# Norm by token after the product: the first layer's inputs reach the multiplier without their square roots

## The chip, the cores and the metric

The kernel runs on one core of one Trainium2 chip. The metric is the device time of one execution in microseconds, the median of several runs. The core's engines work side by side, each in the order of its own program, and meet at semaphores: TensorE (PE in the rows) multiplies, VectorE (DVE), ScalarE (ACT) and GpSimd (POOL) do elementwise work, SyncE (SP) issues most of the DMA transfers.

## What is computed

Two transformer blocks over 256 tokens of 1024 channels. Only the start of the first matters here:

```
def rms_norm(x, g):
    y = xf * lax.rsqrt(jnp.mean(xf * xf, axis=-1, keepdims=True) + EPS)
    return (y * g)
u = rms_norm(h, norm_mix[i])
m = rms_norm(mem, norm_mem[i])
mk, mv = jnp.split(m @ w_mem_kv[i], 2, axis=-1)
q, k, v, f_logit, mq = jnp.split(u @ fox_w_in[j], ...)
q = rms_norm(q.reshape(B, S, FOX_HEADS, HEAD_DIM), fox_g_q[j])
k = rms_norm(k.reshape(B, S, FOX_HEADS, HEAD_DIM), fox_g_k[j])
log_f = jax.nn.log_sigmoid((f_logit + fox_b_f[j]).astype(jnp.float32))
mix = forget_attention(q, k, v, log_f)
mem_out = memory_attention(mq, mk, mv, g_mq[i], g_mk[i])
```

Behind it come the output product, a SwiGLU, a second layer (convolution, memory attention, eight experts of which each token takes two) and the second block. Every `rms_norm` divides a token by the root of its mean square plus EPS = 1e-6. A token's divisor is the same for all its channels.

## The kernel before

**Weights in units.** All dense weights are cut into units of 128 x 2048 fp32 (1 MB) that stream through a ring of six buffers, `raw`. A unit is split into a rounded part `wh` (ScalarE, `split_hi`, line 837) and the rest `wl` (VectorE, `split_lo`, line 2074), in three buffers, and the tokens likewise into `xh` and `xl`. A product is three matmuls a step (lines 1371 to 1373, `exact`): 48 matmuls of 256 columns for one of these first units. SP loads unit n as soon as unit n - 6 is split on VectorE. `split_after(name)` stands in the programs of ScalarE and VectorE and splits the unit three places behind `name`; ScalarE's part of it waits until the product `name` is done, since it takes its buffer.

**The order of the first layer.** The units are mk0 and mv0 (keys and values of the memory), mq0 (queries to the memory), then fq0, fk0, fv0, fq1 and so on, so unit 7 is fk1. PE's program before them: 20 filler matmuls on zeros (`idle_start`, line 1513), the sum of the squares of the memory with a matrix of ones (`norm_sum(0)`, line 1394), 16 more fillers (line 1508), mk0, the sum of the squares of x (`norm_sum(1)`), a two-column product for lambda, mv0, the head sums of mk0 (`head_sum(0)`, line 1431), the gate product (`by_heads`, line 1483) with its transpose by token (line 1531), mq0, and the spread of mk0's head roots over channels (`head_spread(0)`, line 1442). mk0 and mq0 take their tokens tile by tile as they arrive (`ready=arriving(...)`), with k as the outer loop over the eight tiles of 128 channels.

**The norms.** ScalarE squares the tokens (line 854), PE sums them, ScalarE takes the root over all 128 x 256 places (`norm_sd`, line 859), VectorE the reciprocal (line 2100) and then the product token x weight x reciprocal, tile by tile (`norm_raw`, line 2067); ScalarE rounds each tile (`norm_hi`, line 880) and VectorE subtracts. `qk_square`, `head_sum`, `qk_sd` (line 902), a reciprocal with a copy (lines 2150 and 2151) and `head_spread` do the same by head behind each of the eight products of queries and keys; `values_out` (line 913) takes a value product out of PSUM. ScalarE's `slot(h)` puts these steps beside the attention, two slots to a unit.

**Side work.** `rn_mem`, the memory's reciprocals, is used once more far behind, for the second layer's memory. The gates go ScalarE, VectorE, ScalarE, then as negated sums to DRAM and back to all partitions on GpSimd's own queue (lines 711 and 700), where GpSimd adds masks (line 707). Ahead of unit 7, SP also writes zeros over `x_rows` and `y_rows` in DRAM (`zero_rows`, lines 637 and 639, 6 MB and 2.5 MB).

## Time and profile before

| what | value |
|---|---|
| median of three runs | 1816.58 us (1816.5 to 1817.22) |
| the profiled execution | 1819.06 us |
| its span, first to last instruction | 1817.2 us |
| mean granted TensorE clock | 0.989 of full |
| busy: PE, VectorE, ScalarE, GpSimd | 98%, 78%, 64%, 13% |

The profile is one execution. It has a page with busy times and groups of instructions, and a trace that can be asked for a timeline, for stretches and for single lines. PE records each fp32 matmul twice, so its counts are double. In a timeline neighbours of the same kind are merged, and the time in brackets is the idle time ahead. An engine's wait counts only where PE, in the end, waits for it.

### The profile page before, as it was taken

What the parts mean: (1) busy time and instruction counts of PE and PEld (TensorE: products, weight loads), DVE (VectorE), ACT (ScalarE), POOL (GpSimd) and SP (SyncE); (2) the same over time, 40 slices, a digit from 0 to 9 for tenths busy, and PEclk for the clock granted to TensorE, in tenths of its full rate; (3) what the DMA queues carried; (4) which work ended last, traced back from release to release, by engine and by line L of the source; (5) the groups of instructions that cost most, each with busy time, mean ns of one, the idle gap of its engine ahead of it and who ended that gap; (6) DMA issues with size and microseconds to landing.
All of it is one profiled execution on the core that took longest, in us unless ns stands there. A gap on an engine that the chain in (4) does not pass through costs nothing.

```text
span 1817.2 us, 28018 instructions
## 1 busy us (share of the span) xinstructions
PE 1788.5 (98%) x10770; PEld 1589.9 (87%) x10770; DVE 1412.7 (78%) x1342; ACT 1164.4 (64%) x1148; POOL 232.5 (13%) x194
## 2 busy tenths in 40 slices
PE   9999999999999999999999999999999999899998
PEld 8988999998988888888888888888887899799998
DVE  6665977689778888888888889888889867665554
ACT  6775434457677777777777777777777767543332
POOL 0452111302030000000000000000007002302221
PEclk9999999999999999999999999999999999999999
DMA  9734888841379999999999999999999953235540
GB/s 392 274 121 139 323 337 324 319 147 35 128 280 383 368 387 376 368 396 373 386 390 365 389 382 367 388 372 396 375 363 422 381 186 139 87 119 179 180 158 24
DMA packets 75695, 523.27 MB, mean 288 GB/s; under 512 B 8328, under 2 KB 8480, under 8 KB 15072
## 3 DMA queue, kind: packets, MB, share of 16 engines
q1 hardware_dynamic: 73344, 514.02, 74.1%
q0 software_dynamic: 2272, 8.15, 1.2%
q8 instruction: 56, 0.92, 0.2%
q14 instruction: 23, 0.19, 0.0%
HBM read 506.38 MB, written 15.75 MB: 287 GB/s over the span
## 4 chain that ended last, share of the span: by engine, by line
PE 92%; DVE 4%; ACT 2%; issue 1%; DMA 0%; POOL 0%; DVEq 0%; SPq 0%; ACTq 0%
PE ps L1371 27%; PE ps L1373 27%; PE ps L1372 27%; PE ps L1704 2%; DVE wl L2074 2%; PE ps L1863 1%; PE ps L1385 1%; PE ps L1552 1%; DVE sqz L2067 1%; ACT wh L837 1%; PE ps L1569 1%; PE ps L1401 0%; PE ps L1394 0%; DMA big<-in_mem 0%; PE ps L1871 0%
## 5 line engine op out<-in xcount | busy, mean ns | idle before, releaser
L2074 DVE TENSOR_TENSOR wl<-raw,wh 128x2048 fp32r<-128x2048 f32 x446 | 1026.6, 2304 | 251.5 <-ACT wh L837 138.8
L1189 ACT ACTIVATE wh<-raw 128x2048 fp32r<-128x2048 f32 x335 | 642.8, 1919 | 179.3 <-PE ps L1373 179.3
L1371 PE MATMUL ps<-wh,xh 128*128 128x512 f32 (+1 forms) x1040 | 396.5, 381 | 2.4 <-DVE wl L2074 2.4
L1373 PE MATMUL ps<-wh,xl 128*128 128x512 f32 (+1 forms) x1040 | 390.1, 375 | 0.0
L1372 PE MATMUL ps<-wl,xh 128*128 128x512 f32 (+1 forms) x1040 | 389.6, 375 | 0.0
L1371 PE MATMUL ps<-xh,wh 128*128 128x256 f32 x1120 | 323.1, 288 | 5.5 <-DVE xl L2074 3.7
L1372 PE MATMUL ps<-xl,wh 128*128 128x256 f32 x1120 | 318.5, 284 | 0.0
L1373 PE MATMUL ps<-xh,wl 128*128 128x256 f32 x1120 | 318.5, 284 | 0.0
L837 ACT ACTIVATE wh<-raw 128x2048 fp32r<-128x2048 f32 x108 | 206.3, 1911 | 174.4 <-PE ps L1373 170.6
L1371 PEld LDWEIGHTS ps<-wh,xh 128*128 128x128 f32 x1040 | 195.8, 188 | 38.8 <-DVE wl L2074 4.0
L1373 PEld LDWEIGHTS ps<-wh,xl 128*128 128x128 f32 x1040 | 195.7, 188 | 35.7
L1372 PEld LDWEIGHTS ps<-wl,xh 128*128 128x128 f32 x1040 | 196.0, 188 | 34.0 <-issue 0.5
L1371 PEld LDWEIGHTS ps<-xh,wh 128*128 128x128 f32 x1120 | 216.7, 193 | 9.4 <-issue 6.8
L1372 PEld LDWEIGHTS ps<-xl,wh 128*128 128x128 f32 x1120 | 216.5, 193 | 0.5 <-issue 0.5
L1373 PEld LDWEIGHTS ps<-xh,wl 128*128 128x128 f32 x1120 | 216.4, 193 | 0.0
L1371 PE MATMUL ps<-wh,ah 128*128 128x512 f32 x448 | 175.8, 392 | 0.0
L1373 PE MATMUL ps<-wh,al 128*128 128x512 f32 x448 | 174.6, 390 | 0.0
L1372 PE MATMUL ps<-wl,ah 128*128 128x512 f32 x448 | 174.5, 389 | 0.0
L1371 PE MATMUL ps<-ah,wh 128*128 128x256 f32 x496 | 142.4, 287 | 1.0 <-POOL al L747 0.9
L1372 PE MATMUL ps<-al,wh 128*128 128x256 f32 x496 | 140.8, 284 | 0.0
L1373 PE MATMUL ps<-ah,wl 128*128 128x256 f32 x496 | 140.8, 284 | 0.0
L747 POOL TENSOR_TENSOR al<-att_p,ah 128x512 fp32r<-128x512 f32 x27 | 74.6, 2762 | 333.9 <-ACT ah L1051 333.9
(327 smaller groups left out, 1960.8 us busy)
## 6 DMA issues: line engine op xcount, KB each, us to landing
raw<-in_experts SPq DMA_DIRECT2D x336, 1024.0 KB, 6.8
raw<-in_units SPq DMA_DIRECT2D x134, 1024.0 KB, 5.3
x_rows<-big SPq DMA_DIRECT2D x1, 6144.0 KB, 35.6
big<-x_rows SPq DMA_DIRECT2D x8, 512.0 KB, 7.8
y_rows<-big SPq DMA_DIRECT2D x7, 512.0 KB, 8.2
y_rows<-big SPq DMA_DIRECT2D x1, 2560.0 KB, 41.3
sqz<-gate_rows POOLq DMA_DIRECT2D x12, 192.0 KB, 4.4
big<-in_mem SPq DMA_DIRECT2D x1, 1024.0 KB, 7.1
```

What stands on the lines that cost most here:

```text
L747: pool.tensor_tensor(al[:, c % 2, :], sg[:, c % 2, :], ah[:, c % 2, :].bitcast(F32), ALU.subtract).then_inc(sem("hid_lo"), 1)
L837: act.activation(wh[:, p % SPL, :], raw[:, n % RAW, :], ACT.Copy).then_inc(sem("hi_ready"), 1)
L1189: act.activation(wh[:, p % SPL, :], raw[:, n % RAW, :], ACT.Copy).then_inc(sem("hi_ready"), 1)
L1371: mm(out_, lh, rh, start=start, stop=False, **kw)
L1372: mm(out_, lh, rl, start=False, stop=False, **kw)
L1373: return mm(out_, ll, rh, start=False, stop=stop, **kw)
L1385: ins = pe.transpose(bank(name)[:, at:at + P], src, ident)
L1552: ins = mm(s[:, at:at + nk], m["q"][:, P * t:P * t + P], m["k"][:, 0:nk], start=True, stop=True)
L1569: mm(o, m["v"][0], pT[:, 0:T], start=True, stop=False, skip_group_check=True)
L1704: mm(bank(f"conv{c}")[:, 0:T], diag[:, n % DIAG_RING, :], upad[:, c, tap:tap + T], start=(tap == 0), stop=(n + 1 == taps_through(PE_CONV, ...
L1863: ins = pe.transpose(psum[:, P * f:P * f + P], sg[:, c % 2, P * f:P * f + P], ident)
L2074: return V.tensor_tensor(out_, whole, leading.bitcast(F32), ALU.subtract)
```

## The change

The first layer no longer divides tokens before the products. `xh` and `xl` are made from token x norm weight alone: ScalarE's `weighted_hi` rounds that product, VectorE's `weighted_lo` subtracts. What was left out is a factor by token, and it is put back where a token's row is small:

- queries and keys are normed by head anyway, so there the factor cancels except in EPS; `qk_sd` now adds EPS x (mean square + EPS) by token (`tok_eps`) and takes two instructions, one for each half of the tokens;
- values (`values_scaled_out`, two instructions for one) and gate logits (VectorE, two for one) are multiplied by the token's reciprocal `tok_r`;
- the sums of squares come by token (four matmuls of one column each for x and the memory) behind mv0, of squares that VectorE has added up first; the squares of the memory are GpSimd's, which did nothing there before, those of x ScalarE's;
- the gate product takes x itself against weights times norm weights (`gate_w`), by token at once: 16 matmuls of 12 columns in place of 8 of 256 and a transpose;
- `rn_mem`, needed later, comes from two more transposes on PE and a copy on ScalarE.

mk0's and mv0's units and the memory are loaded, split and multiplied in halves, the load order is new (`cols` early, the constants late), the second filler is gone and the first has 18 matmuls.

```diff
-            load(0)
-            sp.dma_start(flat(mem0), mem_dram).then_inc(sem("ld_mem"), 16)
+            first = main_dram[0:1, :, :].rearrange("a p f -> p (a f)")
+            sp.dma_start(raw[:, 0, 0:HALF], first[:, 0:HALF]).then_inc(sem("first_half_loaded"), 16)
+            sp.dma_start(cols[:, :], cols_dram).then_inc(sem("ld_cols"), 16)
+            sp.dma_start(flat(mem0)[:, 0:HALF], mem_dram[:, 0:HALF]).then_inc(sem("ld_mem"), 16)
+            sp.dma_start(raw[:, 0, HALF:UW], first[:, HALF:UW]).then_inc(sem("ring_loaded0"), 16)
+            sp.dma_start(flat(mem0)[:, HALF:UW], mem_dram[:, HALF:UW]).then_inc(sem("ld_mem_rest"), 16)
+            load(1)
+            sp.dma_start(flat(hT), x_dram).then_inc(sem("ld_x"), 16)
             sp.dma_start(cst[:, 0:C_ROT], cst_dram[:, 0:C_ROT]).then_inc(sem("ld_cst"), 16)
-            sp.dma_start(cols[:, :], cols_dram).then_inc(sem("ld_cols"), 16)
-            sp.dma_start(flat(hT), x_dram).then_inc(sem("ld_x"), 16)
...
+            for j in range(4):
+                pool.wait_ge(sem("ld_mem" if j < 2 else "ld_mem_rest"), 16)
+                pool.tensor_tensor(sqz[:, 512 * j:512 * j + 512], pair_of(mem0, j), pair_of(mem0, j),
+                                   ALU.mult).then_inc(sem("mem_sq"), 1)
...
+            def split_hi_half(p, half):
+
+                if (p, half) == (0, 0):
+                    act.wait_ge(sem("first_half_loaded"), 16)
+                else:
+                    wait_loaded(act, p)
+                at = slice(HALF * half, HALF * half + HALF)
+                act.activation(wh[:, p, at], raw[:, p, at], ACT.Copy).then_inc(
+                    sem("hi_ready" if half else "hi_half_ready"), 1)
...
+            def weighted_hi(src, at, k):
+
+                act.activation(xh[:, k, :], src[:, k, :], ACT.Copy,
+                               scale=cols[:, at + k:at + k + 1]).then_inc(sem("norm_hi"), 1)
...
+                    act.activation(rq[:, k % 2, :], bank(f"qsum{k}")[:, 0:8], ACT.Sqrt, scale=1.0 / HD,
+                                   bias=eps).then_inc(drained(f"qsum{k}"), 1)
+                    return
+                of = int(k > 0)
+                act.wait_ge(sem("tok_eps_ready"), of + 1)
+                roots, sums = (v.rearrange("p (a t n) -> p a t n", a=2, t=TT)
+                               for v in (rq[:, k % 2, :], bank(f"qsum{k}")[:, 0:8]))
+                for t in range(TT):
+                    ins = act.activation(roots[:, :, t, :], sums[:, :, t, :], ACT.Sqrt, scale=1.0 / HD,
+                                         bias=tok_eps[:, of, t:t + 1])
+                ins.then_inc(drained(f"qsum{k}"), 1)
...
+            def values_scaled_out(name, dst, of):
+
+                wait_done(act, name)
+                act.wait_ge(sem("tok_r_ready"), 1)
+                for t in range(TT):
+                    ins = act.activation(dst[:, t, :], bank(name)[:, T * t:T * t + T], ACT.Copy,
+                                         scale=tok_r[:, of, t:t + 1])
+                ins.then_inc(drained(name), 1)
...
+            split_hi_half(0, 0)
+            act.wait_ge(sem("ld_cols"), 16)
             act.wait_ge(sem("ld_mem"), 16)
+            for k in range(2):
+                weighted_hi(mem0, V_MEM, k)
+            split_hi_half(0, 1)
+            for k in range(2, KT):
+                if k == 4:
+                    act.wait_ge(sem("ld_mem_rest"), 16)
+                weighted_hi(mem0, V_MEM, k)
+            split_hi_half(1, 0)
+            split_hi_half(1, 1)
+            act.wait_ge(sem("ld_x"), 16)
             for j in range(4):
-                square(mem0, sqz, j)
+                act.activation(x_sq[:, 512 * j:512 * j + 512], pair_of(hT, j), ACT.Square).then_inc(sem("norm_sq"), 2)
+            split_hi(2)
             act.wait_ge(sem("ld_cst"), 16)
             warm(ACT.Sqrt)
-            norm_sd(0, rn_mem)
-            norm_hi("mem0", mem0)
-            act.wait_ge(sem("ld_x"), 16)
-            for j in range(4):
-                square(hT, x_sq, j)
-            split_hi(1)
-            norm_sd(1, rn)
-            split_hi(2)
             qk_square(0)
             split_after("mk0")
             wait_done(act, "mv0")
-            norm_hi("x")
-            wait_filled(act, "foxf")
-            act.activation(forget, bank("foxf")[0:FOX_HEADS, 0:T], ACT.Copy).then_inc(drained("foxf"), 1)
+            for k in range(KT):
+                weighted_hi(hT, V_MIX, k)
+            qk_sd(0)
+            act.wait_ge(sem("tok_eps_ready"), 2)
+            act.activation(flat(tok_r), flat(tok_ms), ACT.Sqrt).then_inc(sem("tok_sd"), 1)
             split_after("mv0")
             wait_filled(act, "nsum1")
-            values_out("mv0", vv[:, :, FOX:D])
-            qk_sd(0)
+            values_scaled_out("mv0", vv[:, :, FOX:D], 0)
...
+                        values_scaled_out(name, vv[:, :, at:at + T], 1)
                     if h == 5:
                         qk_spread(0)
+                        wait_filled(act, "memr")
+                        act.activation(rn_mem[:, :], bank("memr")[:, 0:T], ACT.Copy).then_inc(drained("memr"), 1)
                     elif FOX_UNITS[u - 1] in QK_UNITS:
                         qk_spread(QK_UNITS.index(FOX_UNITS[u - 1]))
                     split_after(name)
                 if h == 7:
...
                 claim(pe, name)
                 steps = [(t, k) for k in range(KT) for t in range(2)] if ready else [(t, k) for t in range(2) for k in range(KT)]
                 for t, k in steps:
+                    if halves and (t, k) == (0, KT // 2):
+                        pe.wait_ge(sem("lo_ready"), POS[name] + 1)
...
-            for _ in range(20):
+            for _ in range(18):
                 mm(bank("idle_start")[:, 0:P], idle_tile, idle_tile, start=True, stop=True)
+            by_channels("mk0", ready=arriving("mem0"), halves=True)
+            by_tokens("mv0", halves=True)
+
             pe.wait_ge(sem("ld_cst"), 16)
-            norm_sum(0)
-            keep_running("idle_mem0", 16)
-            by_channels("mk0", ready=arriving("mem0"))
-            norm_sum(1, x_sq)
-
+            claim(pe, "nsum1")
+            pe.wait_ge(sem("x_sq_added"), 3)
+            for c in range(2):
+                ins = add_by_token(1, c, x_sq, 0, 1)
+            ins.then_inc(filled("nsum1"), 1)
+            claim(pe, "nsum0")
+            pe.wait_ge(sem("mem_sq_added"), 3)
+            for c in range(2):
+                ins = add_by_token(0, c, sqz, 0, 1)
+            ins.then_inc(filled("nsum0"), 1)
+            claim(pe, "flT")
+            pe.wait_ge(sem("gate_w_ready"), 1)
+            pe.wait_ge(sem("ld_x"), 16)
+            for k in range(KT):
+                for t in range(TT):
+                    at = FOX_HEADS * t
+                    ins = mm(bank("flT")[:, at:at + FOX_HEADS], hT[:, k, P * t:P * t + P], gate_w[:, k, :],
+                             start=(k == 0 and t == 0), stop=(k == KT - 1), skip_group_check=True)
+            ins.then_inc(filled("flT"), 1)
+            head_sum(0)
             pe.wait_ge(sem("lam_prod"), 2)
             claim(pe, "lam")
             mm(bank("lam")[:, 0:2], ones, lam[:, 0:2], start=True, stop=True).then_inc(filled("lam"), 1)
-            by_tokens("mv0")
-            head_sum(0)
-
-
-            pe.wait_ge(sem("ld_cols"), 16)
-            by_heads("foxf", cols[:, V_WF:V_RT].rearrange("p (k n) -> p k n", k=KT), FOX_HEADS, "x")
-            claim(pe, "flT")
-            for t in range(TT):
-                ins = mm(bank("flT")[:, FOX_HEADS * t:FOX_HEADS * t + FOX_HEADS], forget[:, P * t:P * t + P],
-                         ident[0:FOX_HEADS, 0:FOX_HEADS], start=True, stop=True)
-            ins.then_inc(filled("flT"), 1)
+
             by_channels("mq0", ready=arriving("x"))
             head_spread(0)
+            claim(pe, "memr")
+            pe.wait_ge(sem("tok_r_ready"), 1)
+            for t in range(TT):
+                ins = pe.transpose(bank("memr")[:, P * t:P * t + P], tok_r[:, 0, t:t + 1].broadcast_to([P, P]), ident)
+            ins.then_inc(filled("memr"), 1)
...
+                dve.wait_ge(sem("hi_ready" if half else "hi_half_ready"), p + 1)
+                at = slice(HALF * half, HALF * half + HALF)
+                rest(wl[:, p, at], raw[:, p, at], wh[:, p, at]).then_inc(
+                    sem("lo_ready" if half else "lo_half_ready"), 1)
...
+            def weighted_lo(name, src, at, k):
+
+                wait_hi(dve, name, k)
+                stt(xl[:, k, :], src[:, k, :], col(at + k), xh[:, k, :].bitcast(F32), ALU.mult,
+                    ALU.subtract).then_inc(sem("norm_lo_dve"), 1)
...
+            def token_means(k, of):
+
+                wait_filled(dve, f"nsum{k}")
+                V.tensor_scalar(tok_ms[:, of, :], bank(f"nsum{k}")[:, 0:TT], 1.0 / D, EPS, ALU.mult,
+                                ALU.add).then_inc(drained(f"nsum{k}"), 1)
+                wait_drained(dve, f"nsum{k}")
+                V.tensor_scalar(tok_eps[:, of, :], tok_ms[:, of, :], EPS, None, ALU.mult).then_inc(sem("tok_eps_ready"), 1)
...
-            split_lo(0)
+            split_lo_half(0, 0)
             dve.wait_ge(sem("ld_cols"), 16)
+            for k in range(2):
+                weighted_lo("mem0", mem0, V_MEM, k)
+            split_lo_half(0, 1)
+            for k in range(2, KT):
+                weighted_lo("mem0", mem0, V_MEM, k)
+            split_lo_half(1, 0)
+            split_lo_half(1, 1)
+            V.tensor_tensor(gate_w, cols[:, V_WF:V_RT].rearrange("p (k n) -> p k n", k=KT),
+                            cols[:, V_MIX:V_MIX + KT].unsqueeze(2).broadcast_to([P, KT, FOX_HEADS]),
+                            ALU.mult).then_inc(sem("gate_w_ready"), 1)
+            for j in (1, 2, 3):
+                dve.wait_ge(sem("norm_sq"), 2 * (j + 1))
+                if j > 1:
+                    dve.wait_ge(sem("x_sq_added"), j - 1)
+                V.tensor_tensor(x_sq[:, 0:512], x_sq[:, 0:512], x_sq[:, 512 * j:512 * j + 512],
+                                ALU.add).then_inc(sem("x_sq_added"), 1)
+            for j in (1, 2, 3):
+                dve.wait_ge(sem("mem_sq"), j + 1)
+                if j > 1:
+                    dve.wait_ge(sem("mem_sq_added"), j - 1)
+                V.tensor_tensor(sqz[:, 0:512], sqz[:, 0:512], sqz[:, 512 * j:512 * j + 512],
+                                ALU.add).then_inc(sem("mem_sq_added"), 1)
+            split_lo(2)
...
-            split_lo(1)
-            norm_rms(1, rn)
-            norm_raw(hT, gains(V_MIX), rn[:, :])
-            split_lo(2)
-            norm_lo("x")
+            for k in range(2):
+                weighted_lo("x", hT, V_MIX, k)
+            token_means(0, 0)
+            token_means(1, 1)
+            for k in range(2, KT):
+                weighted_lo("x", hT, V_MIX, k)
             split_after("mk0")
+            dve.wait_ge(sem("tok_sd"), 1)
+            V.reciprocal(flat(tok_r), flat(tok_r)).then_inc(sem("tok_r_ready"), 1)
+            head_root(0)
...
             wait_filled(dve, "flT")
-            V.tensor_tensor(lsf[:, 0, :, :], bank("flT")[:, 0:2 * FOX_HEADS].rearrange("p (a b) -> p a b", a=2),
-                            cols[:, V_BF:V_BF + FOX_HEADS].unsqueeze(1).broadcast_to([P, TT, FOX_HEADS]),
-                            ALU.add).then_inc(drained("flT"), 1)
+            dve.wait_ge(sem("tok_r_ready"), 1)
+            for t in range(TT):
+                ins = stt(lsf[:, 0, t, :], bank("flT")[:, FOX_HEADS * t:FOX_HEADS * t + FOX_HEADS], tok_r[:, 1, t:t + 1],
+                          cols[:, V_BF:V_BF + FOX_HEADS], ALU.mult, ALU.add)
+            ins.then_inc(drained("flT"), 1)
```

The first rows of PE's program. Before, `ps<-sqz,cst` is the first sum of squares and `ps<-cst` the second filler:

```order
L1513 MATMUL ps<-att_pT 128x128 x20
L1394 MATMUL ps<-sqz,cst 128x256 x8
L1508 MATMUL ps<-cst 128x128 x16
L1371 MATMUL ps<-xh,wh 128x256
L1372 MATMUL ps<-xl,wh 128x256
L1373 MATMUL ps<-xh,wl 128x256
```

The same place in the changed kernel, with the semaphores that each row waits for:

```order
L1553 MATMUL ps<-att_pT 128x128 [waits idle_tile]
L1553 MATMUL ps<-att_pT 128x128 x17
L1421 MATMUL ps<-xh,wh 128x256 [waits norm_lo_dve,lo_half_ready]
L1422 MATMUL ps<-xl,wh 128x256
L1423 MATMUL ps<-xh,wl 128x256
L1421 MATMUL ps<-xh,wh 128x256
```

The sum and the second filler went from ahead of the first product, which now waits for half a unit (`lo_half_ready`) and a tile (`norm_lo_dve`).

PE's program between mv0 and mq0. Before, `att_pT` holds the squares of mk0, `cols` the gate weights and `att_p` the gate product:

```order
L1371 MATMUL ps<-wh,xh 128x256
L1372 MATMUL ps<-wl,xh 128x256
L1373 MATMUL ps<-wh,xl 128x256
L1431 MATMUL ps<-cst,att_pT 128x2 x4
L1483 MATMUL ps<-sqz,cols 12x256 x8
L1531 MATMUL ps<-cst,att_p 128x12 x2
L1371 MATMUL ps<-xh,wh 128x256
```

The same place in the changed kernel, where `big` and `sqz` hold the added squares of x and of the memory and `plan_f` the weighted gate weights:

```order
L1422 MATMUL ps<-wl,xh 128x256
L1423 MATMUL ps<-wh,xl 128x256
L1445 MATMUL ps<-cst,big 128x1 x4
L1445 MATMUL ps<-cst,sqz 128x1 x4
L1574 MATMUL ps<-plan_f,hT 128x12 x16
L1475 MATMUL ps<-cst,att_pT 128x2 x4
L1580 MATMUL ps<-lam,cst 128x2
L1421 MATMUL ps<-xh,wh 128x256
```

The sums by token stand here now, the gate product has 16 small matmuls and no transpose, and the lambda product came down from ahead of mv0.

VectorE's program from its start. Before, `gq` and `lam` are small constants and `rn_mem` the memory's reciprocals:

```order
L2074 TENSOR_TENSOR wl<-raw,wh 128x2048
L2171 TENSOR_SCALAR gq<-cols 128x1
L2172 TENSOR_SCALAR gq<-cols 128x2
L2174 TENSOR_TENSOR lam<-cols 128x1
L2175 TENSOR_TENSOR lam<-lam,cst 128x1
L2176 TENSOR_TENSOR lam<-lam,cst 128x1
L2100 RECIPROCAL rn_mem<-rn_mem 128x256
L2067 SCALAR_TENSOR_TENSOR big<-big,cols,rn_mem 128x256 x3
L2074 TENSOR_TENSOR xl<-big,xh 128x256
L2067 SCALAR_TENSOR_TENSOR big<-big,cols,rn_mem 128x256
```

The same place in the changed kernel:

```order
L2127 TENSOR_TENSOR wl<-raw,wh 128x1024
L2120 SCALAR_TENSOR_TENSOR xl<-big,cols,xh 128x256 x2
L2127 TENSOR_TENSOR wl<-raw,wh 128x1024
L2120 SCALAR_TENSOR_TENSOR xl<-big,cols,xh 128x256 x6
L2127 TENSOR_TENSOR wl<-raw,wh 128x1024 x2
L2251 TENSOR_TENSOR plan_f<-cols 128x96
L2258 TENSOR_TENSOR big<-big 128x512 x3
L2264 TENSOR_TENSOR sqz<-sqz 128x512 x3
L2127 TENSOR_TENSOR wl<-raw,wh 128x2048
L2268 TENSOR_SCALAR gq<-cols 128x1
```

The tiles of the memory come directly behind half a unit, without a reciprocal, and six additions of squares came in ahead of the next whole unit.

## Rows read from the trace of the kernel before

**Rows 1.** the page, first part: busy us, share of the span, instructions
```profile
PE 1788.5 (98%) x10770; PEld 1589.9 (87%) x10770; DVE 1412.7 (78%) x1342; ACT 1164.4 (64%) x1148; POOL 232.5 (13%) x194
```

**Rows 2.** PE's timeline: start us, us, engine line op out<-in xcount
```profile
0.97 7.33 PE L1513 MATMUL ps<-att_pT 128*128 128x128 f32 x40 [0.97 <-POOL att_pT L693]
9.02 3.69 PE L1394 MATMUL ps<-sqz,cst 128*128 128x256 f32 x16 [0.72 <-ACT sqz L854]
16.80 0.55 PE L1371 MATMUL ps<-xh,wh 128*128 128x256 f32 x1 [2.34 <-DVE xl L2074]
...
24.07 3.62 PE L1394 MATMUL ps<-big,cst 128*128 128x256 f32 x16
...
33.51 0.95 PE L1431 MATMUL ps<-cst,att_pT 128*128 128x2 f32 x8
34.38 3.62 PE L1483 MATMUL ps<-sqz,cols 128*12 128x256 f32 x16
...
39.01 0.39 PE L1371 MATMUL ps<-xh,wh 128*128 128x256 f32 x1
...
44.87 0.60 PE L1442 MATMUL ps<-cst,rq_by_head 128*128 128x128 f32 x4
...
51.95 0.60 PE L1442 MATMUL ps<-cst,rq_by_head 128*128 128x128 f32 x4
...
69.45 0.60 PE L1442 MATMUL ps<-cst,rq_by_head 128*128 128x128 f32 x4
```

**Rows 3.** stretches: span, busy of each engine (x), PEclk, DMA share, GB/s
```profile
19.00:20.00 1.00, 1.00 (x7) 1.00 (x6) 1.00 (x4) 0.42 (x1) 0.00 (x0) 0.50 1.02 426
20.00:21.00 1.00, 1.00 (x10) 1.00 (x10) 0.98 (x3) 0.99 (x3) 0.00 (x0) 0.95 1.03 426
```

**Rows 4.** timelines of ScalarE and SP, one DMA issue (KB, us to landing)
```profile
5.75 1.91 ACT L837 ACTIVATE wh<-raw 128x2048 fp32r<-128x2048 f32 x1 [3.75 <-DMA raw<-in_units]
8.24 2.19 ACT L854 ACTIVATE sqz<-big 128x512 f32<-128x512 f32 x4 [0.59 <-DMA big<-in_mem]
...
10.86 21.50 SPq L639 DMA_DIRECT2D y_rows<-big  x1
...
raw<-in_units SPq DMA_DIRECT2D x1, 1024.0 KB, 22.2
```

**Rows 5.** GpSimd's L747 (duration min/median/max ns), then timelines of both
```profile
L747 POOL TENSOR_TENSOR al<-att_p,ah x27: 1288/2879/2889, 185.6 to 1796.9; 128x512 fp32r<-128x512 f32 x27
...
201.98 2.63 POOL L747 TENSOR_TENSOR al<-att_p,ah 128x512 fp32r<-128x512 f32 x1 [13.53 <-ACT ah L1051]
203.74 3.01 DVE L2074 TENSOR_TENSOR wl<-raw,wh 128x2048 fp32r<-128x2048 f32 x1 [0.30 <-ACT wh L837]
...
357.79 2.31 DVE L2074 TENSOR_TENSOR wl<-raw,wh 128x2048 fp32r<-128x2048 f32 x1 [3.10 <-ACT wh L837]
357.91 2.78 POOL L690 TENSOR_TENSOR xl<-sqz,xh 128x256 fp32r<-128x256 f32 x1
```

**Rows 6.** timelines of four engines, one row of DMA issues
```profile
30.02 3.26 DVE L2067 SCALAR_TENSOR_TENSOR sqz<-hT,cols,rn 128x256 f32<-128x256 f32 x8
...
33.71 2.56 ACT L880 ACTIVATE xh<-sqz 128x256 fp32r<-128x256 f32 x8 [1.41 <-PE ps L1373]
...
61.82 1.92 ACT L837 ACTIVATE wh<-raw 128x2048 fp32r<-128x2048 f32 x1
...
66.16 1.28 ACT L902 ACT_TABLE_LOAD   x1
...
sqz<-gate_rows POOLq DMA_DIRECT2D x5, 192.0 KB, 5.5
...
67.96 3.93 POOL L707 TENSOR_TENSOR sqz<-sqz,cst 128x128 f32<-128x128 f32 x10 [3.29 <-DMA sqz<-gate_rows]
...
68.45 0.57 DVE L2151 COPY rq_by_head<-rq 128x512 f32<-128x512 f32 x1
...
74.48 0.60 PE L1385 MATMUL ps<-cst,att_p 128*128 128x128 f32 x4
```

More of the change, by code:

```diff
@@ L640, in zero_rows @@
                              zeros.broadcast_to([P, MAXBLK + 2 - E, D])).then_inc(sem("rows_zeroed"), 16)
-            for n in range(1, U0):
+            for n in range(2, U0):
                 if n == NUMBER["fk1"]:
@@ L1444, in head_spread, with by_channels @@
                 ins.then_inc(filled(f"qrms{k}"), 1)
-            def by_channels(name, nb=None, ready=None, half_done=None):
-                h, l = weights(name, KT, nb)
+            def by_channels(name, nb=None, ready=None, half_done=None, halves=False):
+                h, l = weights(name, KT, nb, halves)
                 claim(pe, name)
@@ L1470, in by_tokens @@
                     for k in range(KT):
+                        if halves and (t, k) == (0, KT // 2):
+                            pe.wait_ge(sem("lo_ready"), POS[name] + 1)
                         c = slice(P * t, P * t + P)
```

51 lines of the change are left out of this document (19 added, 32 removed).

## The prediction

> **What bounds the kernel now.** I read the busy times first: PE is busy for 1788.5 of 1817.2 us [rows 1], so time can come only from PE instructions that vanish and from the 28.7 us in which PE has none. The change touches the first 75 us, so next came PE's timeline from the start. The filler of 20 small matmuls (40 records, the hardware runs each in two) ends at 8.3, the sum of the memory's squares runs from 9.02 to 12.7, a second filler to 14.5, then PE has nothing for 2.3 us, and the first product, mk0, starts only at 16.80 [rows 2]. Ahead of it lie the square root, the reciprocal and the multiplication by it. After mk0 comes the sum of the squares of x at 24.07, then mv0, the head sums at 33.51, the gate product of 3.62 us at 34.38, a wait and its transpose until 39.01, where mq0 starts; the spread behind mq0 stands at 44.87, the next two that I use at 51.95 and 69.45 [rows 2]. From 39 to 69.45 PE has no gap. The granted clock is 0.50, so 1.2 GHz, in mk0's first 3.2 us, just after the 2.3 us of nothing: still 0.50 from 19 to 20 and 0.95 from 20 to 21, with 7 matmuls in the one stretch and 10 in the other [rows 3]. So a burst after a gap has two prices.
>
> **The front of mk0.** Weights and tokens come over one DMA queue: ScalarE starts on the first MB at 5.75 and on the second at 8.24, both released by their DMA [rows 4], so 2.5 us per MB. In the new order that gives half a unit at 4.5, the columns at 5.1, half the memory at 6.4, the second halves at 7.7 and 8.9, unit 1 at 11.4, x at 13.9 and unit 2 at 16.9. The total up to unit 2 is the old one.
> ScalarE rounds 2048 columns in 1.92 and eight tiles of 256 in 2.56 [rows 6], so it has the first half at 5.5, tiles 0 and 1 by 7.1, the second half at 8.7 and tile 7 at 10.7. VectorE takes 2.3 for 2048 columns [rows 5] and 0.41 per tile (3.26 for eight [rows 6]). Alone it would have tile 0 at 7.4, tile 1 at 7.8, the second half at 10.0, tile 2 at 10.4, tile 7 at 12.5.
> It isn't alone: the four squares of the memory go to GpSimd. A 128x512 tile takes it 1.29 at least, 2.88 in the median [rows 5]. The rows show why: the tile that started at 201.98 took 2.63, and the VectorE split beside it, started at 203.74, took 3.01 in place of 2.31; the GpSimd tile at 357.91 took 2.78, until the split of 357.79 had ended [rows 5]. One waits for the other's whole instruction, and the one already waiting goes next. So I let them alternate: square 0 at 6.7 to 7.95 (behind the first weight half), tile 0 to 8.4, square 1 to 9.65, tile 1 to 10.1, square 2 to 11.35, second half to 12.5, square 3 to 13.75, tile 2 to 14.2, tile 7 at 16.2. Had GpSimd run all four first, tile 2 would stand at 14.2 too.
> The Trainium skill (SBUF — State Buffer, section "SBUF: two separate sides") says the same and goes further: GpSimd and a VectorE instruction with two SBUF inputs exclude each other for a whole instruction. The trace agrees for the splits (2.78, 3.01); by that rule the line above holds for the new tiles too, and without it tile 2 would come at 10.4.
> PE's filler of 18 ends at 7.6 (7.33 x 36/40 from 0.97 [rows 2]). Tiles 0 and 1 are short bursts at 8.4 and 10.1, then PE waits some 3.3 us for tile 2. Before, 2.3 us of nothing brought the clock down, so I take the low clock from 14.2: 15 matmuls of 0.21 in 3.2 us, as from 16.80 to 20.0 [rows 2, 3], and 21 at 0.12 (5.86 per 48, from 39.01 to 44.87 [rows 2]). **mk0 ends at 19.9**, before at 24.07. At full clock it would be 18.5, without the collisions at 14.7 to 16.3.
>
> **From mk0 to mq0.** mv0 needs unit 1 split, at 18.5, so it runs from 19.9 to 25.8. Then 8 matmuls for the two sums by token and 16 for the gates, all bound by loading 128x128 fp32 weights: 0.20 each, by the four of the head sum, which fill 33.51 to 34.38 with some overlap [rows 2]: 1.6 and 3.2. Bounds for the 16: the same as the old eight with 256 columns, 3.62, and 0.12 each, 1.9. Head sum 0.8, lambda 0.3. **mq0 starts at 31.6, before 39.01: 7.4 earlier.** Gone from PE between mk0 and mq0 are the second sum (24.07, 3.62), the gate product (3.62) and 1.0 of wait and transpose [rows 2]; the first sum and the fillers stood ahead of mk0 and are paid in its start.
> Is x ready? VectorE: unit 1 to 18.5, gate weights, six additions of 512 columns at about 0.7 (estimate from 2.3 for 2048) to 22.9, unit 2 to 25.2. ScalarE rounds x behind mv0's end, 25.8 to 28.4; VectorE's last x tile is at 31.1 at 0.41 each, behind the sums by token at 27.6. mq0 takes 0.73 per tile, so it isn't held.
>
> **What is late next.** ScalarE's queue: root for heads 31.6, unit 4 32 to 34, values 34.7 (two instructions for one, about +0.2), three table loads of 1.28 [rows 6] with the exponential and the logarithm to 39.0, squares of mq0 39.5, spread 40.0, the new copy of the memory's reciprocals 40.3, unit 5 42.2, table 43.5, root 43.9. VectorE splits unit 5 until 44.5, reciprocal and copy to 45.1. PE has mq0 to 37.5, spread 0.4, the two new transposes 0.3, fq0 and head sum to 44.7, and waits about 0.4. Its spread stands at 45.2 where it stood at 51.95 [rows 2]: **6.8 earlier**.
> The second limit is a DMA. The zeroing of y_rows blocks SP from 10.86 for 21.50 us; unit 7 is issued only then, at 32.4, and lands 22.2 later, at 54.6 [rows 4]. Nothing in the change moves these bytes: the DMA engines are full (share 1.02 [rows 3]), before and after. ScalarE starts unit 7 at 61.82 [rows 6], so it can be at most 7.2 earlier. Behind that, in order, are table loads, the root of fk0, and VectorE's copy of 0.57 at 68.45 [rows 6], which ends 0.4 ahead of PE's spread at 69.45 [rows 2]; the root is now two instructions, about +0.2. **PE can be at most about 7.4 earlier there, however fast the front is.** At 6.8 the unit is wanted at 55.0 and just doesn't wait.
> GpSimd: ten masks of gates from 67.96 take 3.93, loaded 5.5 us after issue [rows 6], and everything on that path moves with the 6.8.
> Later stages: PE waits there for its own producers, no load, so the 6.8 stays. The two-part roots and values add about 0.2 on ScalarE seven and four times; I count 0.
>
> **The sum.** The profiled execution took 1819.06 (span 1817.2), 2.5 above the median 1816.58: 1819.06 - 6.8 = 1812.3, and for the median **1809.8**.
>
> **Rivals.** (1) Forecast, 55%: 6.8, with 5.6 to 7.3 for the unknown prices (flT 1.9 to 3.6, ScalarE's added instructions): 1809.3 to 1811.0.
> (2) The collisions cost less or the clock stays up, 20%: for it, the alternation is inferred from single cases; against it, four of four squares meet busy VectorE. mq0 starts at 26.5 to 30, and unit 7 stops the gain at 7.4: 1809.2.
> (3) Neither limit holds, 6%: unit 7 lands earlier as the halves change the queue, and mq0 starts at 26.5. Gain 11 to 12: about 1805. Against it: same bytes, same queue, full at both ends.
> (4) ScalarE and VectorE queues slip more, 15%: each further us at the chain from mq0's squares to 45.1 is a us of PE, since there PE already waits. With 1.5 to 3.8 us more: gain 3.0 to 5.3, 1811.3 to 1813.6.
> (5) Slower, 4%: the gate loads. They are issued at about 55 in place of 61.9, with more ring loads open. If they queue behind these, they land as unit 7 does [rows 4], some 20 us after issue, at 75.5; masks take 3.9, and from their end at 71.9 it was 2.6 to the first transposes of probabilities at 74.48 [rows 6]. These then stand at 82, where PE wants them at 67.7: 14 us lost against 6.8 won, 1824. It decides from a landing of about 13 us on. Against it: before, while the engines were full, they landed in 5.5 [rows 6].
>
> **Chances and range.** About 0.2% (3.6 us) can be told from no change here: faster, below 1812.9, holds (1) to (3) and most of (4): 0.91; same 0.05; slower 0.04. For 8 in 10 the range takes in (1), (2) with 1.4 us for unit 7's landing, which the smaller packets may move, and most of (4), and leaves out (3) and (5): 1807.8 to 1812.6.
>
> **What would show it.** After: mk0's first matmul at 8 to 9 and tile 2's at about 14; POOL's four squares 1.3 to 2.6 each; granted clock 0.50 from about 14; mq0 at 31.6; a short wait of PE before the spread at 45; unit 7 landing at 54.6 and wanted then. A start of mq0 below 29 with the same total would prove (2); a total below 1807 would prove my unit 7 limit wrong; PE waits of over 1 us between 38 and 55 would speak for (4).

## The result and the profile after it

| | kernel before | changed kernel |
|---|---|---|
| median of 20 runs, us | 1816.59 (1813.92 to 1821.23) | 1819.16 (1816.53 to 1824.66) |
| ratio to the kernel before, 95% interval | | 1.0016 (1.0010 to 1.0023) |
| span of the profiled execution, us | 1817.2 | 1819.1 |

The forecast was 1809.8, within 1807.8 to 1812.6. The changed kernel takes 2.6 us **more**. The interval excludes a gain. The loss is small, but a second series (e12, below) gave 1.0025 (1.0014 to 1.0035).

**The front did what was forecast.** PE's timeline of the changed kernel from the start (start, us, engine, line, operation, shapes, count, in brackets the idle time before it and what ended it):

```profile
0.97 5.84 PE L1553 MATMUL ps<-att_pT 128*128 128x128 f32 x36 [0.97 <-POOL att_pT L700]
8.75 0.36 PE L1421 MATMUL ps<-xh,wh 128*128 128x256 f32 x1 [1.94 <-DVE xl L2120]
...
13.22 0.39 PE L1421 MATMUL ps<-xh,wh 128*128 128x256 f32 x1 [2.40 <-DVE xl L2120]
...
25.35 0.95 PE L1445 MATMUL ps<-cst,big 128*128 128x1 f32 x8
26.16 1.03 PE L1445 MATMUL ps<-cst,sqz 128*128 128x1 f32 x8
27.06 5.99 PE L1574 MATMUL ps<-plan_f,hT 128*128 128x12 f32 x32
32.89 1.84 PE L1475 MATMUL ps<-cst,att_pT 128*128 128x2 f32 x8
34.60 0.56 PE L1580 MATMUL ps<-lam,cst 128*128 128x2 f32 x2
42.35 0.60 PE L1486 MATMUL ps<-cst,rq_by_head 128*128 128x128 f32 x4
...
49.65 0.60 PE L1486 MATMUL ps<-cst,rq_by_head 128*128 128x128 f32 x4
...
67.16 0.60 PE L1486 MATMUL ps<-cst,rq_by_head 128*128 128x128 f32 x4
...
77.01 1.11 PE L1438 MATMUL ps<-cst,att_p 128*128 128x128 f32 x4 [4.37 <-POOL att_p L736]
```

mk0 starts at 8.75 in place of 16.80 [rows 2], memory tile 2 comes at 13.22 (forecast 14.2), mk0 ends at 19.6 (forecast 19.9), and mv0 ends at 25.35 (forecast 25.8). Then the 16 short gate matmuls (32 records) take 5.99 us, the head sum 1.84 and the lambda product 0.56, and the spread behind mq0 stands at 42.35. That is 2.5 us ahead of the 44.87 of before [rows 2], and the lead is 2.3 at the other two spreads (49.65 against 51.95, 67.16 against 69.45). Then PE stands still for 4.37 us in front of the first transposes of probabilities: they come at 77.01, before at 74.48 [rows 6].

The stretches show the clock in both places. Columns: from and to; PE, its weight loads, VectorE, ScalarE and GpSimd busy, each with its number of instructions; granted clock, DMA share, GB/s:

```profile
26.00:28.00 2.00, 2.00 (x20) 2.00 (x19) 0.95 (x3) 2.00 (x5) 0.00 (x0) 1.00 1.01 422
28.00:30.00 2.00, 2.00 (x12) 2.00 (x12) 1.96 (x8) 1.78 (x5) 0.00 (x0) 0.54 0.97 401
30.00:32.00 2.00, 2.00 (x11) 2.00 (x11) 2.00 (x4) 0.00 (x0) 0.00 (x0) 0.50 1.02 420
32.00:35.00 3.00, 3.00 (x15) 3.00 (x16) 1.01 (x1) 0.22 (x2) 0.00 (x0) 0.50 1.03 425
35.00:38.00 3.00, 3.00 (x15) 3.00 (x16) 1.58 (x4) 2.98 (x7) 0.00 (x0) 0.50 1.02 421
38.00:42.00 4.00, 4.00 (x34) 4.00 (x34) 2.06 (x5) 3.02 (x5) 0.00 (x0) 0.95 1.02 417
70.00:76.00 6.00, 2.62 (x17) 1.96 (x15) 4.44 (x6) 2.08 (x5) 4.44 (x7) 0.99 0.27 72
76.00:80.00 4.00, 2.99 (x14) 2.99 (x15) 1.51 (x4) 0.86 (x2) 2.89 (x5) 0.50 0.56 233
```

From 28 to 38 PE is counted as busy all the time, and runs at 0.50, that is 1.2 GHz. From 76 to 80, behind the wait, it is at 0.50 again.

What GpSimd does in front of those transposes, in the changed kernel's timeline of POOL:

```profile
60.17 2.75 POOL L710 DMA_DIRECT2D sqz<-gate_rows  x5 [5.57 <-DMA gate_rows<-rn]
66.64 0.78 POOL L717 TENSOR_TENSOR sqz<-sqz,cst 128x128 f32<-128x128 f32 x2 [3.71 <-DMA sqz<-gate_rows]
...
71.16 0.78 POOL L717 TENSOR_TENSOR sqz<-sqz,cst 128x128 f32<-128x128 f32 x2 [0.61 <-DMA sqz<-gate_rows]
72.89 2.25 POOL L717 TENSOR_TENSOR sqz<-sqz,cst 128x128 f32<-128x128 f32 x2 [0.95 <-DMA sqz<-gate_rows]
75.12 0.93 POOL L734 TENSOR_SCALAR att_p<-att_p,rsum 128x256 f32<-128x256 f32 x1
76.04 0.92 POOL L736 TENSOR_SCALAR att_p<-att_p,rsum 128x256 f32<-128x256 f32 x1
```

and VectorE's weight split beside the last of them:

```profile
72.23 2.27 DVE L2127 TENSOR_TENSOR wl<-raw,wh 128x2048 fp32r<-128x2048 f32 x1
```

The gate loads are issued at 60.17, 1.7 us earlier than the 61.91 of before, but land one by one, 6.3 to 10.5 us after issue (median 8.4, before 5.4 to 5.9). The last pair of masks begins at 72.89, inside VectorE's split of 72.23 to 74.50, and takes 2.25 us where the others take 0.78. The normalisation of map 0's probabilities stands behind it on GpSimd: 75.12 to 76.96. PE wanted it at 72.64. Before, the masks ran from 67.96 to 71.9 [rows 6], the normalisation until 73.70, VectorE's split began at 74.13 and PE came at 74.48: everything fitted, with 0.8 us to spare for PE and 0.4 for the split. These are the two normalisations and the split of before:

```profile
71.86 0.94 POOL L724 TENSOR_SCALAR att_p<-att_p,rsum 128x256 f32<-128x256 f32 x1
72.78 0.92 POOL L726 TENSOR_SCALAR att_p<-att_p,rsum 128x256 f32<-128x256 f32 x1
...
74.13 2.27 DVE L2074 TENSOR_TENSOR wl<-raw,wh 128x2048 fp32r<-128x2048 f32 x1
```

### The profile page after: what moved, and what is told of

Its sections match the earlier page's. It is cut to its first block, busy times and chain, and to the rows that moved or that the text cites. A ratio compares the mean times of both kernels' runs of the same rounds, so it can differ in the third digit from the quotient of the medians.

```text
span 1819.1 us, 27999 instructions
## 1 busy us (share of the span) xinstructions
PE 1784.5 (98%) x10748; PEld 1588.2 (87%) x10748; DVE 1411.5 (78%) x1339; ACT 1164.9 (64%) x1157; POOL 237.5 (13%) x198
## 4 chain that ended last, share of the span: by engine, by line
PE 90%; DVE 4%; ACT 2%; DMA 1%; issue 1%; POOL 1%; DVEq 0%; SPq 0%; ACTq 0%
PE ps L1421 27%; PE ps L1423 27%; PE ps L1422 27%; DVE wl L2127 2%; PE ps L1757 2%; PE ps L1916 1%; PE ps L1438 1%; ACT wh L847 1%; DMA sqz<-gate_rows 1%; DVE sqz L2120 1%; PE ps L1622 1%; PE ps L1605 0%; PE ps L1445 0%; DMA raw<-in_units 0%; PE ps L1924 0%
## 5 line engine op out<-in xcount | busy, mean ns | idle before, releaser
L2127 DVE TENSOR_TENSOR wl<-raw,wh 128x2048 fp32r<-128x2048 f32 (+1 forms) x448 | 1027.1, 2295 | 248.6 <-ACT wh L847 129.4
```

The lines of the kernel that those rows point to most:

```text
L2127: return V.tensor_tensor(out_, whole, leading.bitcast(F32), ALU.subtract)
```

## The experiments

One measure needs a word first. From 154 us on the kernels run the same instructions, but spells of low clock fall in other places of them in each execution, and the profiled runs drift against each other by some us until the end. Two late stretches of the kernel before, and then of the changed kernel:

```profile
1480.00:1500.00 20.00, 20.00 (x166) 19.89 (x165) 10.78 (x11) 12.26 (x14) 1.21 (x4) 1.00 0.46 159
1580.00:1600.00 20.00, 17.52 (x125) 16.57 (x124) 8.90 (x24) 8.19 (x25) 6.54 (x6) 0.91 0.16 54
```

```profile
1480.00:1500.00 20.00, 20.00 (x157) 19.89 (x157) 12.63 (x17) 11.20 (x13) 0.00 (x0) 0.94 0.36 113
1580.00:1600.00 20.00, 16.18 (x120) 14.77 (x118) 9.81 (x32) 9.32 (x29) 8.95 (x9) 1.00 0.16 54
```

The granted clock is below 1 in the second stretch of the one and in the first of the other. So the table has, beside medians and ratios, the time in the profile at which GpSimd issues the load of c_row, behind the first attention. It is a reading of one execution. The three kernels that should agree there do: before 154.42, e1 154.45, e11 154.39. Two executions of one kernel differ by more: 0.35 for the changed kernel (159.77 and 159.42), 0.81 for e4 and e8, which are the same.

| run | gate product, us | first spread | PE waits for probabilities | c_row load | median, us | ratio (95%) |
|---|---|---|---|---|---|---|
| before | 3.62 | 44.87 | 0 | 154.42 | 1816.4 to 1817.2 | 1 |
| after | 5.99 | 42.35 | 4.4 | 159.77 | 1819.16 | 1.0016 (1.0010 to 1.0023) |
| e12 after again | 6.23 | 42.09 | 4.4 | 159.42 | 1821.67 | 1.0025 (1.0014 to 1.0035) |
| e1 before, zeroing late | | 44.90 | 0 | 154.45 | 1815.66 | 0.9987 (0.9977 to 0.9998) |
| e2 after, zeroing late | 3.90 | 40.24 | 0 | 150.54 | 1814.09 | 0.9980 (0.9969 to 0.9991) |
| e3 gates by heads | 3.62 | 39.64 | 4.4 | 155.74 | 1817.96 | 1.0002 (0.9991 to 1.0012) |
| e4, e8 e2 and e3 | 3.62 | 36.67, 37.47 | 0 | 146.97, 147.78 | 1810.29, 1810.41 | 0.9958 (0.9942 to 0.9974), 0.9957 (0.9941 to 0.9974) |
| e5 wide gates | 3.79 | 38.97 | 4.4 | 155.37 | 1818.63 | 1.0000 (0.9988 to 1.0012) |
| e6 by heads, ring held | 3.62 | 37.61 | 4.4 | 155.08 | 1818.00 | 1.0002 (0.9990 to 1.0013) |
| e7 e8, squares late | 3.62 | 38.09 | 0 | 148.46 | 1811.18 | 0.9963 (0.9949 to 0.9977) |
| e9 after, probabilities first | 3.72 | 39.50 | 0 | 149.80 | 1815.44 | 0.9987 (0.9974 to 0.9999) |
| e10 e3, probabilities first | 3.62 | 38.16 | 0 | 148.46 | 1811.28 | 0.9968 (0.9959 to 0.9977) |
| e11 before, probabilities first | | 44.84 | 0 | 154.39 | 1815.62 | 0.9998 (0.9988 to 1.0008) |

(Gates "by heads" are eight matmuls of 12 stationary and 256 streamed columns, as in the kernel before, instead of 16. The changed kernel's gate product is 16 matmuls of 12 streamed columns; e2 and e9 have it unchanged, e5 streams 96. Each median is of 6 to 20 executions, each ratio is to executions of the kernel before on the same chip, and can differ by 0.001 from the quotient of the medians, as in e5.)

### First four: the queue and the clock

The profile left two theories. Q: the DMA engines are full with the zeroing of rows and the weights, so the gate loads land late however early they are asked for. C: the clock falls in the short gate matmuls. e1 and e2 move the zeroing behind later weight loads, in the kernel before and in the changed one:

```
-                if n == NUMBER["fk1"]:
+                if n == NUMBER["fo0"] + 1:
                     zero_rows()
```

> The kernel before, with the zeroing of x_rows and y_rows issued six units later (ahead of unit 13 in place of unit 7). Theory Q (queue): in the first 75 us the DMA engines are full with 8.5 MB of zeros, so whatever needs a transfer there comes at a fixed time however early it is asked for. The kernel before is late enough not to wait for any of it, so this gives the same time, within 0.1% of 1816.6. Rival P (programs): the changed kernel lost its gain on ScalarE, VectorE and GpSimd, the queue has no part; same here too. A gain of over 2 us here would be against both and would mean that the zeroing itself costs PE time.

> The changed kernel with the zeroing issued six units later. Theory Q: the five gate loads land 1.5 us apart no more but within 3 us of their issue, PE's wait of 4.4 us before the first transposes of probabilities goes, with it the low clock behind it (about 2 us), and PE keeps the lead of 2 to 2.5 us that it had at mq0: 1819.2 - 6.2 = 1813, 0.2% below the kernel before. Rival P: the gates are late from ScalarE's or VectorE's order, the wait stays, 1819.

e3 puts the gate product back into the form of before, the 12 gate columns stationary and 256 tokens streamed, with its copy and its transposes; e4 has both edits.

```
-                for t in range(TT):
-                    ins = mm(bank("flT")[:, at:at + FOX_HEADS], hT[:, k, P * t:P * t + P], gate_w[:, k, :], ...)
+                ins = mm(bank("foxf")[0:FOX_HEADS, 0:T], gate_w[:, k, :], hT[:, k, :], ...)
```

> The changed kernel, but the gate product in the old form: 8 matmuls of 256 columns with the weighted gate weights as stationary operand, a copy on ScalarE and the transpose, in place of 16 of 12 columns. Zeroing where it was. Theory C (clock): the 16 short matmuls took 5.9 us since the clock fell to 0.50 in them, and it stayed down into mq0; with 256 columns it stays at 1.00, mq0 starts at 32.5 to 33 in place of 35.0 and its spread stands at 38.8 to 39.5 in place of 42.35. With theory Q the gain is lost again at the gate loads, which land at 70 to 73 as before: total 1818 to 1820. Without Q it would be 1816. Rival to C: the short matmuls are slow by themselves (0.37 us each); then head sum and first half of mq0 are still slow here.

> Both edits: gate product by heads and zeroing late. Theories C and Q together: lead of 5.5 to 6 us at mq0's spread, no wait for gates: 1810.5 to 1811.5, near my forecast for the change. If Q is wrong: as e3.

e3 keeps the clock at 1.00 from 26 to 42, so C holds: the spread comes at 39.64 in place of 42.35. But it ends only level with the kernel before (1.0002), since the wait of 4.4 us is still there. e2 removes the wait; e4 has both gains and stands near the forecast, 6.1 us below the kernel before. But Q was too simple. In e2 the gate loads still took 8.3 us to land. What the late zeroing shortened was the two stores ahead of them (2.2 and 1.9 us to landing in place of 5.2 and 5.8), so that the loads were asked for at 54.13. And e1, in which nothing waited, shows that zeroing late is worth nothing to the chain of the kernel before (154.45).

### Next four: width, order of loads, squares

> The changed kernel, but each of the 16 gate matmuls streams 96 columns instead of 12 (the 12 gate columns eight times over, through a broadcast view; only the first copy is read). The result is the same. Theory C2 (the clock falls because only 12 columns go through behind each 128x128 weight load): with 96 columns the granted clock stays at 1.00 from 26 to 35, the 16 take 3.2 to 3.7 us in place of 5.99, the head sum 1.0 in place of 1.84, mq0 starts at about 32 in place of 35.0. The wait for the gate masks stays (theory Q): landing 8 us, PE waits 3.5 to 5; total 1816.5 to 1818.5. Rival W (what lowers the clock is any run of small matmuls with a new 128x128 stationary each, however wide): clock 0.5 from 28 to 35 again, the 16 take 5.9 or more, mq0 at 35 or later, total as the changed kernel, 1819.

```
-                             gate_w[:, k, :],
+                             gate_w[:, k, :].unsqueeze(1).broadcast_to([P, 8, FOX_HEADS]),
```

The timeline's row and the stretches of e5:

```profile
28.44 3.79 PE L1574 MATMUL ps<-plan_f,hT 128*128 128x96 f32 x32
```

```profile
28.00:30.00 2.00, 2.00 (x20) 2.00 (x20) 1.68 (x8) 2.00 (x6) 0.00 (x0) 1.00 0.97 403
30.00:32.00 2.00, 2.00 (x20) 2.00 (x20) 2.00 (x6) 0.24 (x1) 0.00 (x0) 1.00 1.02 418
32.00:35.00 3.00, 3.00 (x28) 3.00 (x27) 2.41 (x4) 1.92 (x4) 0.00 (x0) 1.00 1.03 423
```

Same weight loads, same count, eight times the columns, and the 16 take 3.79 us against 5.99. C2 holds, W falls. Width itself costs nothing here: in e9 (below) the clock stayed up until all 16 narrow ones were through, and they took 3.72:

```profile
25.92 3.72 PE L1576 MATMUL ps<-plan_f,hT 128*128 128x12 f32 x32
```

```profile
28.00:30.00 2.00, 2.00 (x19) 2.00 (x18) 1.97 (x7) 1.57 (x4) 0.00 (x0) 0.92 0.98 403
30.00:32.00 2.00, 2.00 (x10) 2.00 (x11) 2.00 (x3) 0.79 (x4) 0.00 (x0) 0.50 1.01 416
```

So something that doesn't grow with the columns sets the pace, 0.23 to 0.24 us a matmul at full clock; that it is the load of the 128x128 weights, as the forecast had it, fits but isn't shown by itself. What the width decides is the clock. All four profiles with 12 columns lose it between 27.6 and 30.0 us (changed kernel, e12, e2, e9), and none of the seven with 96 or 256 does. From the first gate matmul to the spread behind mq0 the four take 13.6 to 15.3 us, e5 10.5 and the six by heads 11.2: the low clock costs 3.0 to 4.8 us, by where it falls. Even so e5's median of 1818.63 lies just above its expected range, since its wait of 4.4 us stayed.

> The gate product by heads as in e3, and in addition SyncE issues ring unit 11 and the ones behind it only after the gates are stored, so just about when GpSimd issues its five gate loads; no bytes vanish. Theory R (the gate loads wait behind the ring loads issued ahead of them): they land 5 to 6.5 us after issue instead of 8.1, the last mask ends by 69 instead of 72.5, PE's wait for probabilities falls from 4.4 to 1 to 2.5 us, total 1814 to 1816. Rival Z (the DMA engines are behind by the zeroing and by units 7 to 10 anyway, the order of the last ones doesn't matter): landing 7.5 to 8.5, wait 3.5 to 5 us, total 1817 to 1818. Unit 11 is issued at about 60 and split behind 80, so neither expects a wait for it.

```
+                if n == 11:
+                    sp.wait_ge(sem("gate_stored"), 32)
                 load(n)
```

Landing is 8.4 us in the median, the wait 4.4, the total as in e3: by the expectation R falls. But the edit tests it only weakly. SyncE waits for the same stores as GpSimd, so unit 11 went out at 55.11, 0.3 us ahead of the first gate load, and two ring loads landed among the gate loads at 67.2 and 70.0, as in e3 (67.5 and 70.6). It doesn't exclude that an open ring load slows them (see the end of the next section).

The wait speaks against Z as well. It is 4.37 us to the digit in the changed kernel, e3, e5 and e6:

```profile
74.29 1.12 PE L1442 MATMUL ps<-cst,att_p 128*128 128x128 f32 x4 [4.37 <-POOL att_p L738]
73.64 0.81 PE L1438 MATMUL ps<-cst,att_p 128*128 128x128 f32 x4 [4.37 <-POOL att_p L736]
72.45 1.11 PE L1444 MATMUL ps<-cst,att_p 128*128 128x128 f32 x4 [4.37 <-POOL att_p L740]
```

(These are e3, e5, e6.) Measured from PE's request, the last pair of masks began 0.25 us behind it in the changed kernel, 0.02 ahead in e3, 1.33 behind in e5 and 0.14 behind in e6. A wait that doesn't depend on how late its cause is has another cause.

> e4 (gate product by heads, zeroing late), and GpSimd begins the four squares of the memory only when VectorE has done its eight memory tiles. Theory P (the collisions of GpSimd and VectorE cost the front about 3 us): memory tile 2 is ready at 10.4 to 11 in place of about 13.2, PE's wait on VectorE falls from 4.0 to at most 1.5 us, mk0 ends 2.5 to 4 us earlier. What of that reaches the first spread depends on unit 1's split, which is then late: 1.5 to 3 us there (spread at 34 to 35 against 36.7), total 1807.5 to 1809.5. Rival L (the loads and the splits of units 1, 2 and x set the pace, so the front's gain is given back before mq0): spread at 36 to 37, total as e4, 1810 to 1811.

> e4 once more, as a control for e7 on the same chip and for the size of its lead. If both causes are all that stood between the changed kernel and the forecast: 1809.5 to 1811.5, ratio to the kernel before 0.995 to 0.997. If e4's six runs were lucky draws of the low-clock spells: 1812 to 1814.

P's gain doesn't come. Without the squares beside them the tiles come in one row, and mk0 runs from 10.78 without a break. But it does so at the low clock until 16.9, and its spread comes at 38.09, e8's at 37.47; the median is 1811.18, above P's 1807.5 to 1809.5. In e8, with two waits of 2.37 and 1.66 us, the clock stayed up. What the collisions cost at one and the same clock no run shows. e8 repeats e4.

### Last four: the order on GpSimd

The constant 4.37 pointed at GpSimd's order. Its last masks wait for VectorE's split to end, and the split stands at a fixed place behind map 1's maxima, 0.41 or 0.42 us ahead of PE's request in all four kernels. In the changed kernel PE asks at 72.64, the split ends at 74.50, then what is left of the masks (0.6) and two normalisations (1.84) give 76.96, and PE starts at 77.01. So once the last masks begin while the split runs, it doesn't matter when in it they begin. Maps 0 to 3 need no gate. The edit lets the probabilities go first:

```
             for a in fox_maps:
                 normalise([a])
+                if a == 0:
+                    for h in range(GATES - 1):
+                        mask_gate(h)
+                if a == 1:
+                    mask_gate(GATES - 1)
```

> The changed kernel with one edit in GpSimd's order: the probabilities of attention map 0 are normalised ahead of the gate masks, and those of map 1 ahead of the last gate's mask (maps 0 to 3 are of the memory heads and use no gate). Loads and bytes are as before. Theory O (order and port: the first normalisation is queued behind the last gate's mask, and that mask, begun after VectorE's weight split has started, waits for the split's end; how late the gates land counts only through this): map 0's probabilities are ready at about 68 in place of 76.95, PE's wait of 4.4 us goes, at most 0.5 us is left, and so goes the low clock behind it (0.50 in 76 to 80). Shift against the kernel before at 80 us: -1 to -2 in place of +4. Total 1813 to 1815. Rival M (something else is late there, the wait only changes its name: the next map, the gates' first user at map 4): 2 to 4 us of wait elsewhere before 110 us, total 1817 to 1819.

> e3's gate product by heads (clock kept, first spread at 39.6 in place of 42.35) and e9's order on GpSimd; the zeroing stays where it is. If the two causes, clock and order, are all: no PE wait over 1 us between 40 and 150, e3's lead of 5.2 us kept, total 1810.5 to 1812.5. If the zeroing in front of unit 7 is a cause of its own (unit 7 lands at about 54.6 to 57 and is wanted at about 55 less the 5.2 and more): a wait of 0.5 to 2 us at unit 7, total 1812 to 1814.

> Control: the kernel before with e9's order on GpSimd. There PE doesn't wait for map 0's probabilities (they are ready at 73.70, PE takes them at 74.48), so by theory O the order is worth nothing: 1816 to 1817, ratio 0.999 to 1.001. If the order is worth 2 us or more here too, it is a gain of its own that says nothing of the change.

> Control: the changed kernel once more beside e9, to take the spread between chips out. Its 20 runs gave 1819.16 (1816.5 to 1824.7), ratio 1.0016: expected 1818 to 1820, with the same wait of 4.4 us for GpSimd at 72.6 and the granted clock at 0.50 from 28 to 38.

POOL's timeline in e9:

```profile
57.05 2.75 POOL L710 DMA_DIRECT2D sqz<-gate_rows  x5 [5.30 <-DMA gate_rows<-rn]
63.28 1.17 POOL L730 TENSOR_SCALAR att_p<-att_p,rsum 128x256 f32<-128x256 f32 x1 [3.48 <-DVE rsum L2351]
64.44 0.92 POOL L732 TENSOR_SCALAR att_p<-att_p,rsum 128x256 f32<-128x256 f32 x1
65.34 2.27 POOL L717 TENSOR_TENSOR sqz<-sqz,cst 128x128 f32<-128x128 f32 x6
68.04 0.78 POOL L717 TENSOR_TENSOR sqz<-sqz,cst 128x128 f32<-128x128 f32 x2 [0.43 <-DMA sqz<-gate_rows]
69.56 2.88 POOL L730 TENSOR_SCALAR att_p<-att_p,rsum 128x256 f32<-128x256 f32 x1 [0.74 <-DVE rsum L2351]
```

Map 0's probabilities are ready at 65.3, the gates land as late as before (8.0 us in the median, the last 11.5), and no wait of PE over 1 us is left from 40 to 150. O holds, M falls. e12 and e9, measured on one chip, give the price: 1821.67 and 1815.44, 6.2 us for an order of 10 masks. (Both lie above what was expected of them, 1818 to 1820 and 1813 to 1815.) At the c_row load it is 9.6 us (159.42 against 149.80). That is 4.4 of wait, 2.6 of low clock behind it (the changed kernel is 2.5 us late at the first transposes, 77.01, and 5.1 at the second, 83.58 against 78.46), and 2.6 that e9's profile had more in front by luck, not by its edit: there the clock fell only behind the 16. e11 shows that in the kernel before the order is worth nothing. e10 has nearly the forecast's lead: the first spread comes 6.7 us earlier (38.16 against 44.87), the second 6.5 (45.47 against 51.95, forecast 6.8), the c_row load 6.0, and the median is 5.9 below the kernel before, with the zeroing left where it was.

## The prediction, step by step

- **Front, collisions** (forecast tile 2 at 14.2, mk0's end 19.9, mv0's 25.8): right. GpSimd's squares took 2.22 and 3.10 us for each two, mk0 ended at 19.6 and mv0 at 25.35. In e7's profile the front without collisions was no faster, since the clock fell there.
- **16 short matmuls, 3.2 us; head sum 0.8**: the first term that failed. The base price was near (3.72 for 16 in e9 and 3.79 in e5, at 1.00), and the bounds of 1.9 to 3.6 were drawn from rows at full clock alone. The term had no price for the clock falling inside them, with no gap before it, and that is what the runs showed: 5.99 and 1.84, lambda 0.56, and mq0's first 3.4 us at half speed. Together the spread came at 42.35 where 37.5 was forecast, 4.85 late: 3.4 at mq0's start, 1.4 in mq0.
- **The wait of 0.4 before the second spread, ScalarE's queue, unit 7's cap**: not reached. With mq0 that late nothing else was tight. In e10 and e4 the spread came 6.7 and 8.2 us earlier and no wait arose for ScalarE's chain either, so nothing here speaks for rival (4); the cap of 7.4 held no one back in e10, and in e4 the late zeroing had lifted it.
- **"Everything on that path moves with the 6.8"**: the step that turned the sign. The path over DMA didn't move with its engines: the loads went out 1.7 us earlier and landed up to 10.5 us after issue instead of 5.9, so the masks moved 1.3 us ahead at their first (66.64 against 67.96) and 3.2 us back at their last (75.12 against 71.9), while PE had moved ahead by 1.8. The step named neither what stands behind the masks on GpSimd (the normalisation of map 0, which needs no gate) nor what meets them at the port (VectorE's split, 0.4 us behind the normalisation in the kernel before). In the sum: of the 6.8 us the clock left a lead of 2.5, and the wait with the low clock behind it made of that a lag of 5.1 at the second transposes (83.58 against 78.46).
- **Rival (5)** named this place and the way, gate loads behind full DMA engines. It gave it 4% and priced it by unit 7's 22 us of landing, at 14 us; its 13 us is the landing at which the loss would eat the whole 6.8. By its own numbers a wait begins much sooner: PE wants the transposes at 67.7, masks and the rest take 3.9 and 2.6, so loads issued at about 55 had to land in some 6 us, 0.7 more than the 5.5 on record. That margin was not named. The last load took 10.5 us, and the port did the rest: the bill was 4.4 + 2.6. In the changed kernel, to end ahead of the split at 72.23 the last pair and both normalisations (0.78 + 1.84) had to start at 69.6, 7.2 us behind the last load's issue (72.89 less 10.5).
- **Later stages keep it**: right, at either sign. In sign and within about 3 us the medians keep what the profile has at the c_row load: e10 6.0 there and 5.9 in the median, the changed kernel -5.35 and -2.6, e12 -5.0 and -4.5, e9 4.6 and 1.8. That e4, e8 and e10 come near the forecast number doesn't make it right: they are other kernels, without the two causes that it missed.

The Trainium skill (SBUF — State Buffer, section "SBUF: two separate sides") has the lock of the port by whole instructions; the pair of masks of 2.25 beside the split of 2.27 agrees. In the prediction it was applied to the front and not to the one place where 0.8 us were to spare.

Open: why the five gate loads landed in 5.5 us in the kernel before and e11, and in 8 to 8.5 in all others, which issue them 1.7 to 10 us earlier. The traces show what ran beside them. In the kernel before the last ring load that is open at their issue lands at 67.6, the next is issued only at 66.32, and the five land behind it, at 67.8 to 69.5, 0.3 to 0.5 us apart. In the changed kernel ring loads land among them, at 66.7, 70.2 and 73.4, and the five come at 66.5 to 72.8, 1.4 to 1.8 us apart. In e1 and e2 the zeros of x_rows and y_rows are issued just ahead of them (57.78 and 58.26; 53.35 and 53.82), and they land 1.0 to 1.1 us apart. So sharing the DMA engines with another queue's open transfers would fit every run, and e6, in which ring loads stayed open too, doesn't speak against it; no run tested it by leaving the other queue empty. It isn't known either what made the clock fall at 27.6 or 28.1 in two executions and at 29.7 or 30.0 in two others.

## What carries over

When an engine in order serves both a load of unsure landing and a result that the critical engine wants, put the result first; here the order of ten small masks was worth 6.2 us after the change and nothing before it, since earlier work had used up the slack. Price a step on a DMA path by what else is open on the DMA engines at its new place, not by how far its issue moves. And a run of matmuls with few streamed columns behind full weight loads has two prices, as a burst after a gap has: here it lost the clock, partly for itself and in every case for what stood behind it, and streaming 96 columns where 12 are needed brought the next spread 3.0 to 4.8 us nearer to the first of them.
